# Hybrid decoder layer on one core: W_out's two halves are read back from DRAM once in every block

## The reference

```python
h = rmsnorm(x, norm_g)
proj = h @ w_in                                   # (4096,1024) @ (1024,2576)
q_g, k_g, v_g, gk_lr, gate_g, u_p, gate_p, q_m, gate_m = jnp.split(proj, SPLIT_IDX, axis=-1)
o_gla  = rmsnorm(gla_chunked(q_g, k_g, v_g, gk), gla_norm_g) * silu(gate_g)      # 4 heads, chunks of 64
o_pool = (multiscale_pool(u_p) @ pool_w) * pool_scale * silu(gate_p)             # windows 2, 4, 8, 16
o_mem  = memory_attention(q_m, rmsnorm(mem), w_mem_kv) * silu(gate_m)            # 256 memory tokens
mixed = jnp.concatenate([o_gla, o_pool, o_mem], axis=-1)
x = x + mixed @ w_out                             # (4096,1024) @ (1024,1024)
return rmsnorm(x, final_g)
```

## Time and profile before

| | before |
|---|---|
| median of 3 runs | 1544.04 us (1543.31 to 1545.69) |
| the profiled execution: its span, which is also its own time | 1543.8 us, 0.24 us below the median |
| PE busy | 1443.0 us, 93% |
| DVE, ACT, POOL busy | 47%, 39%, 15% |
| the chain of work that ended last | PE 90% of it, DVE 4%, ACT 2% |
| DVE idle for x's rows (line 883), by the list of waits | 58.5 us in 16 waits, the longest 5.9 us |
| DMA moved | 69.32 MB, mean 45 GB/s |
| one block in the loop | 87.82 us (the same matmuls start at 802.42 us in one block and at 890.24 us in the next) |

### The profile page before, as it was taken

The page is one execution under the profiler, slowest core; times in us unless marked ns, Lnnn a source line. Parts: engine busy times, 40 slices in busy tenths (PEclk is TensorE's granted clock), DMA queues, the critical chain, the costliest instruction groups (busy, mean ns, idle before and its releaser), DMA issues.

```text
span 1543.8 us, 28261 instructions
## 1 busy us (share of the span) xinstructions
PE 1443.0 (93%) x11746; PEld 1046.2 (68%) x11746; DVE 724.0 (47%) x1221; ACT 608.1 (39%) x1101; POOL 236.4 (15%) x217
## 2 busy tenths in 40 slices
PE   3359699999999999999999999999999999999996
PEld 2238476776867677676867677686867767686762
DVE  2876625436172535527163544627163543616253
ACT  1344425344342534434252534434262534434241
POOL 1231201121110201121020202121020112112000
PEclk9669799999999999999999999999999999999998
DMA  8130100102010010102001010202001010201001
GB/s 337 65 136 1 42 2 28 54 0 82 0 69 12 27 54 10 71 0 82 0 36 46 27 54 0 82 0 82 0 27 54 21 61 0 82 0 46 10 28 68
DMA packets 15432, 69.32 MB, mean 45 GB/s; under 512 B 2352, under 2 KB 2480, under 8 KB 12848
## 3 DMA queue, kind: packets, MB, share of 16 engines
q1 hardware_dynamic: 15408, 68.98, 11.9%
HBM read 52.20 MB, written 16.78 MB: 45 GB/s over the span
## 4 chain that ended last, share of the span: by engine, by line
PE 90%; DVE 4%; ACT 2%; DMA 1%; issue 1%; POOL 1%; SPq 1%; DVEq 0%; ACTq 0%; POOLq 0%
PE bank L330 75%; PE bank L484 2%; PE bank L452 2%; PE bank L490 2%; PE bank L476 2%; PE bank L498 2%; DVE whl L852 1%; PE bank L541 1%; DVE wmx L816 1%; PE bank L463 1%; PE bank L388 1%; DMA whl<-in_pool_w 1%; PE bank L435 1%; PE bank L380 1%; POOL arena L1134 1%
## 5 line engine op out<-in xcount | busy, mean ns | idle before, releaser
L330 PE MATMUL bank<-arena,whl 128*128 128x256 f16 x6144 | 684.6, 274 | 2.6 <-DVE whl L852 2.6
L330 PEld LDWEIGHTS bank<-arena,whl 128*128 128x128 f16 x6144 | 602.3, 98 | 84.1 <-issue 6.5
L330 PE MATMUL bank<-arena 128*128 128x512 f16 x1536 | 344.1, 381 | 6.4 <-DVE arena L872 6.4
L330 PEld LDWEIGHTS bank<-arena 128*128 128x128 f16 x1536 | 147.8, 98 | 181.3 <-issue 15.4
L963 DVE SCALAR_TENSOR_TENSOR arena<-arena 64x256 f32<-64x256 f32 x60 | 25.2, 420 | 314.6 <-POOL arena L1191 313.2
L330 PE MATMUL bank<-whl,arena 128*128 128x512 f16 x768 | 168.3, 379 | 0.0
L686 ACT ACTIVATE arena<-bank,sca 128x512 f32<-128x512 f32 x64 | 43.9, 688 | 254.4 <-PE bank L330 253.3
L330 PEld LDWEIGHTS bank<-whl,arena 128*128 128x128 f16 x768 | 75.2, 99 | 86.9
L1143 POOL TENSOR_TENSOR arena<-arena 128x1024 f16<-128x1024 f32 x32 | 77.8, 2451 | 285.7 <-ACT arena L621 285.7
L1134 POOL TENSOR_TENSOR arena<-arena 128x1024 f32<-128x1024 f32 (+2 forms) x48 | 76.7, 1599 | 231.7 <-ACT arena L599 222.6
L1184 POOL TENSOR_TENSOR arena<-arena 128x542 f32<-128x542 f32 x16 | 17.4, 1090 | 606.1 <-ACT arena L693 598.3
(11 more groups left out here) (154 smaller groups left out, 1467.9 us busy)
## 6 DMA issues: line engine op xcount, KB each, us to landing
arena<-in_xt SPq DMA_DIRECT2D x16, 1024.0 KB, 5.2
arena<-in_x SPq DMA_DIRECT2D x32, 512.0 KB, 3.3
out<-arena SPq DMA_DIRECT2D x32, 512.0 KB, 2.6
arena<-in_w_in SPq DMA_DIRECT2D x8, 768.0 KB, 16.1
arena<-in_w_out SPq DMA_DIRECT2D x1, 4096.0 KB, 12.2
arena<-in_w_in SPq DMA_DIRECT2D x8, 392.0 KB, 16.2
arena<-in_w_mem SPq DMA_DIRECT2D x1, 2048.0 KB, 11.0
arena<-in_memt SPq DMA_DIRECT2D x1, 1024.0 KB, 6.6
```

The lines of the kernel that those rows point to most:

```text
L330: mm = nc.tensor.matmul(ap, lhs, rhs, start=k == 0 and n == 0, stop=(k, n) == last)
```

## The change

`wo` gets another layout, so that the half h = 0 or h = 1 of both parts is one contiguous piece of 16 KB in each partition (2 MB in all), and a DRAM tensor `w_out_parts` of 4 MB is added. In block 0, when both parts have been made, SP stores them to DRAM (4 MB), waits for that, and loads both halves back. In each of blocks 1 to 15 SP loads half 0 again after the store of tile 0, when quarter 2 is done, and half 1 after the store of tile 1, when quarter 3 is done. PE waits for half h before quarter h (n = 0 or 1). What is loaded is what the buffer held already. ACT and DVE write the parts in block 0 as two runs of 512 elements instead of one of 1024.

```diff
-        wo = view(O_WO, [2, KT, D], F16)
+        wo = view(O_WO, [2, 2, KT, 512], F16)
+        parts = nc.dram_tensor("w_out_parts", (P, 2, 2 * KT * 512), F16).ap()
...
+                if first:
+                    sp.wait_ge(hi_o, KT)
+                    sp.wait_ge(lo_o, KT)
+                    sp.dma_start(parts, wo.rearrange("p h r k c -> p h (r k c)")).then_inc(d_keep, 16)
+                    sp.wait_ge(d_keep, 16)
+                    for h in range(2):
+                        load(h)
                 if not first:
-                    for t in range(NT):
-                        outputs(i - 1, t)
+                    outputs(i - 1, 0)
+                    reload(i, 0)
+                    outputs(i - 1, 1)
+                    reload(i, 1)
+
+            def load(h):
+
+                sp.dma_start(wo[:, h, :, :, :].rearrange("p r k c -> p (r k c)"), parts[:, h, :]).then_inc(d_wo[h], 16)
+
+            def reload(j, h):
+
+                sp.wait_ge(pe_out, 4 * j - 1 + h)
+                load(h)
...
                 if n >= 2:
                     pe.wait_ge(y_add, 4 * j + n + 3)
+                else:
+                    pe.wait_ge(d_wo[h], 16 * (j + 1))
                 split(bank[h][:, :], KT, lambda k, p, r: (mhl[:, p, k, t * P:(t + 1) * P],
-                                                          wo[:, r, k, h * 512:(h + 1) * 512])).then_inc(pe_out, 1)
+                                                          wo[:, h, r, k, :])).then_inc(pe_out, 1)
```

More of the change, by code:

```diff
@@ L189, in hybrid_block @@
         d_w = [sem(f"d_w{k}") for k in range(KT)]
+        d_keep = sem("d_keep")
+        d_wo = [sem(f"d_wo{h}") for h in range(2)]
         cleared, built, ident_ok, mem_sq, mem_sum, mem_ms, mem_ln, mem_r, mem_n = (
@@ L678, in step @@
                     for k in range(KT):
-                        nc.scalar.activation(wo[:, 0, k, :], woraw[:, k, :], ACT.Copy,
+                        nc.scalar.activation(wo[:, :, 0, k, :], woraw[:, k, :].rearrange("p (h c) -> p h c", h=2), ACT.Copy,
                                              scale=g_out[:, k:k + 1]).then_inc(hi_o, 1)
@@ L951, in step @@
                         dve.wait_ge(hi_o, k + 1)
-                        nc.vector.scalar_tensor_tensor(wo[:, 1, k, :], woraw[:, k, :], g_out[:, k:k + 1],
-                                                       wo[:, 0, k, :], ALU.mult, ALU.subtract).then_inc(lo_o, 1)
+                        nc.vector.scalar_tensor_tensor(wo[:, :, 1, k, :], woraw[:, k, :].rearrange("p (h c) -> p h c", h=2), g_out[:, k:k + 1],
+                                                       wo[:, :, 0, k, :], ALU.mult, ALU.subtract).then_inc(lo_o, 1)
                 if not first:
```

## The result

| | before | changed |
|---|---|---|
| median of 6 runs | 1544.87 us (1543.31 to 1546.04) | 1593.84 us (1590.60 to 1603.16) |
| ratio | | 1.0327, 95% interval 1.0299 to 1.0355 |
| span of the profiled execution | 1543.8 us | 1601.4 us (its own time 1603.16, the longest of the six) |
| DMA moved | 69.32 MB | 140.64 MB |

The account below looks back on a forecast made before the run. PE was taken to bound the kernel, busy for all 87.80 us of a loop block. 21.0 us in the loop plus 3.6 us in the last block gave 24.6 us on 1543.8: 1568 us, range 1547 to 1580.

Parts of the forecast that it names:

- The place and the order: At block ends, half 0's reload precedes x's rows of tile 1 in SP's in-order queue, so `rows(2)` starts 3.7 us late.
- the term of the loop: PE stalls 1.5 us at the end of each of blocks 1 to 14: 21.0 us in all.
- the clock, put at nothing: Matmuls after each new PE stall were taken to run at full clock, adding 0 us to the sum.
- That rival: Clock falls at each new PE stall, costing another 14 x 1.7 = 23 us: 1591 us; chance 0.07.
- A stall is the lateness of x's rows less 2.1 us.: At block ends, a slack of 2.1 us absorbs part of the rows' 3.7 us lateness; PE stalls 1.6, taken as 1.5.
- The last block, 3.6 us.: In the last block the lateness of x's rows passes through undiminished to PE's tail: + 3.6 us.
- The reload of half 1: Issued before `xb`, it makes `xb` land 5 us later, under over 35 us of cover: nothing.
- block 0: Store and loads of 4 MB each finish at about 162 us, before SP's next issue at 185.47: nothing.
- PE's waits: Two new waits for W_out's halves per block, met long before: nothing; at most 0.1 us each, 3 us in all.
- the traffic: Transfers running beside PE's matmuls do not slow them, 5.34 us without and 5.35 with: nothing.
- The tail's last reload: Half 1's last reload and x's last rows land with 0.9 us of slack: nothing, up to 1 us if missed.
- the row of 419: Trace rate of the megabyte issued behind W_out, 419 GB/s; used to price the second megabyte at 2.5 us.

Follow-up runs that it names:

- e1: Changed kernel with SP loading x's rows of tile 1 before half 0 of W_out instead of behind it, same traffic: 1545.59 us.
- e12: The changed kernel itself run once more, nothing altered, as a yardstick: 1596.10 us.
- e9: Changed kernel, but 1 MB of input xt is read ahead of x's rows and half 0 is loaded behind them: 1547.38 us.
- e10: Kernel before, no reload; SP holds back x's rows of tile 1 in blocks 1 to 14, one 16 KB load in front: 1606.81 us.
- e3: Changed kernel with 9 idle matmuls on PE at the start of every block but the first, filling its waits: 1585.21 us.
- e6: Changed kernel with half 0 reloaded as 1.5 MB instead of 2 MB ahead of x's rows: 1568.91 us.
- e4: Changed kernel with W_out's parts stored and loaded back in block 0 only, no reload in the loop: 1545.63 us.
- e8: Changed kernel with half 0 loaded from ScalarE's queue when the store of tile 0 is issued; x's rows stay on SP's: 1625.90 us.
- e11: Changed kernel with half 0 loaded from ScalarE's queue once the store of tile 0 has landed, beside x's rows on SP's: 1616.65 us.
- e7: Changed kernel with half 0's 2 MB read as two transfers of 1 MB, both ahead of x's rows: 1602.41 us.

## Why the prediction was wrong

The place and the order were right and the slack nearly so. Two steps failed: the term of the loop was too small, and the clock, put at nothing, fell. That rival had been given 7 in 100, and its 1591 us lies near the measured 1593.84 in part by luck, since it had stalls of 1.5 us with a fall at each of 14, where the runs have longer stalls and fewer falls.

- **Where.** PE's new waits stand at the start of `features` and of the low-rank projection, with DVE's `add_rows` as releaser, and the 2 MB go out 0.5 us after the store. e1 shows that this order is the whole cause.
- **"A stall is the lateness of x's rows less 2.1 us."** Nearly: 2.0 us late gave none, 3.6 gave 1.3 a block, 4.6 gave 2.3, so it is 2.3 by PE's waits and 2.2 by the length of a block.
- **The term of the loop, 14 x 1.5 = 21.0 us: mis-sized.** The rows were 10.78 us behind the store's issue (10.61 in e12), not 9.9. The runs share the 0.9 us out: 1 MB of W_out's parts costs 8.11 us and not the 7.6 that I took from the place where `xb` is in front (0.5; of it 0.4 by the source, e9); the second megabyte costs 2.7 instead of 2.5 in this profile (0.2), though in e12 it costs 10.61 - 8.11 = 2.5, so this part is within the spread; and the 0.2 us for the earlier issue of the load weren't there. Behind a slack, such an error of 0.9 in 9.9 is one of 0.8 in 1.5: the term came to 30.3 us in e12 and 32.6 in the profile of the change.
- **The last block, 3.6 us.** 4.5, the same lateness, passed on undiminished as said.
- **The clock, 0 us in the sum: wrong.** "It is less than half as long" as the stall at block 1, I wrote against the rival. The stalls were longer than I had them (2.3 against 1.5 us), and at that size most were followed by the lower clock: 14.9 us in e12, 18.4 in the profile of the change. e10 shows that the stall alone does it, e3 that keeping PE busy prevents it. e6 shows that at waits near those I had forecast (1.3 us in the mean, 1.64 at most) there is no fall: nothing for the clock was right for the stall of the sum, and wrong for the stall that came. So the first error brought the second with it. Without the falls the time would still lie just above 1580, the end of the range: 1596.12 - 14.9 = 1581.2 us for e12.
- **The reload of half 1, block 0, PE's waits, the traffic: nothing.** Held (e4, e1). The tail's last reload had been given 0.9 us of slack: DVE's first `rows` of the tail still waits for PE and not for x.
- **The Trainium skill's 358 GB/s** (DMA: Bandwidth & Descriptors, Bandwidth), weighed against the row of 419: the second megabyte took 10.78 - 8.11 = 2.7 us, 393 GB/s, in one profile and 2.5 us, 419 GB/s, in the other of the same kernel; the page's figure would give 2.9. The measurements are on the side of the row.

The spread of the runs, 1590.6 to 1603.2 us, comes in large part from the number of fallen clocks. The mean granted clock of an execution goes from 0.967 at 1590.6 us to 0.960 at 1603.2, though not in strict order, and 0.007 of 1600 us is 11 us of the 12.6 (an estimate). Of the two executions with a profile the one with a span of 1594.4 us has 9 and that with 1601.4 has 11, 3.5 us of the 7.0; another 2.3 us are waits.

## What to carry to other kernels

A transfer that is free as traffic can cost 3% by its place in a queue: before adding one, find the transfer behind it that an engine already waits for, and put the new one behind that. A second queue was no way around a large transfer here (e8, e11). Where a slack swallows most of a delay, give the rest a wide range, since the small difference of two large numbers carries all their error, and if it keeps PE idle, price the matmuls after it at the lower clock too.

## What was not expected of the hardware

- The clock fell after PE had been kept idle twice, for example 1.02 and 1.30 us, with 0.62 us of matmuls between: in 11 of 14 block starts of the changed kernel (waits of 1.92 to 2.95 us in sum), in 9 of 14 of e12 (1.27 to 2.54), in 14 of 14 of e10 (2.35 to 2.80), in none of e6 (0.72 to 1.64). The length of the waits doesn't settle it: falls followed 1.93 us in e12 and 1.79 in e7, none followed 2.54 in e12 and 2.76 in e7. What does is open, and two executions of one program differ by it.
- The lower clock comes when PE is already at work again (0.68 in the mean of 278 to 280 us, PE back at 278.30; 0.50 from 280 to 282), and 48 matmuls take 7.08 us and not 5.41.
- A 0.5 MB store issued within 0.01 us of a 2 MB load from another queue landed after 7.8 us instead of 2.6.
